# k and q of each group of four heads computed in turn, two groups inside the loop over the heads

## The chip, the cores and the metric

The kernel runs on one core of a Trainium2 chip. The metric is the time on the device in microseconds (us), lower is better. A core has TensorE (PE, matrix products; PEld is its loading of weights), VectorE (DVE), ScalarE (ACT), GpSimd (POOL) and SyncE (SP), which here only issues the loads of weights. They run side by side and meet at semaphores; each takes its own instructions strictly in order.

## What is computed

Two networks in a row on x (512 tokens, 1024 channels, float32). The first block is retention and pooling with an FFN; the second is a state space layer with an FFN, and then a layer of latent attention with an FFN. The change is in the attention layer and, by some small table work, in the FFN ahead of it:

```python
ckv = h @ w_kv_a                                   # 288 wide: 256 latent, 32 rope
c_kv = rms_norm(ckv[..., :256], kv_a_norm)
k_rope = apply_rope(rms_norm(ckv[..., 256:], k_rope_norm), cos, sin)
kv = (c_kv @ w_kv_b).reshape(b, s, 16, 128)        # per head: 64 of k, 64 of v
k_nope = rms_norm(kv[..., :64], k_nope_norm); v = kv[..., 64:]
c_q = rms_norm(h2 @ w_q_a, q_a_norm)               # 384 wide
q = (c_q @ w_q_b).reshape(b, s, 16, 96)            # per head: 64, and 32 of rope
q = concat(rms_norm(q[..., :64]), apply_rope(rms_norm(q[..., 64:]), cos, sin))
o = softmax(mask(q @ k.T / sqrt(96))) @ v          # 16 heads
x = x + o @ w_o
```

## The kernel before

Products are made in three passes from operands split in a high and a low part. A weight chunk is loaded by SP (`w_raw`), ACT makes its high part (`w_hi`, L935; for `kv_a` and `q_a` it also multiplies in the gain, L930), POOL the low part (`w_lo`, L864). ACT works up to LEAD = 4 chunks ahead of the one that TensorE is at (`ahead`), and there are six buffers for chunks. Results stand in eight PSUM banks that are used in turn; a bank can be opened when its last user is done. `rows_product` opens four banks (one for each block of 128 tokens, a tile) and goes chunk by chunk over all four; `rows_by_tile` goes tile by tile.

The attention layer runs in this order on TensorE:

1. `kv_a` (288 wide, by tile, chunks of two k) and `q_a` (384 wide, by chunk). DVE copies each result to SBUF (L1829, L1838), ACT makes the mean squares of the copy and their roots (L1190 to L1201), DVE scales (L1836, L1844). Ahead of the first of these DVE makes the angles of rope (L1821 to L1437) and ACT their sines (L1185, L1186).
2. The latents are turned (L461), scaled by their gains and split (DVE L1330, ACT L951, DVE L1299).
3. The columns: for group c = 0 to 3 (four heads each) the product `kv_b` (512 wide, two k, 24 matmuls), then for c = 0 to 3 the product `q_b` (384 wide, three k, 36 matmuls). For each tile ACT squares the result and copies it to `k_n` or `q_n` (L1232, L1234), DVE sums the squares (L1903 to L1907) and copies v (L1910). When all tiles of one product are in, ACT takes the roots (`row_deviations`, L1211, L1213) and DVE normalises (`normalised`: L1873 to L1893). Rope of q is done by POOL for groups 0 and 2 (`rope_queries`, six instructions of `rope_chunk`, L836 to L841, in POOL's queue of low parts), and by DVE inside `normalised` for groups 1 and 3.
4. The heads. Loop h does on TensorE: for each tile t the scores of head h+1 (L749) and the turning of the probabilities of head h (L759); then the turning of q and k of head h+2 (L741), and the output of head h (`head_out`, L768: ten blocks, four of them for the last tile). DVE masks the scores and takes the maxima (L1922) and copies turned probabilities of tiles 0 to 2 (`p_t`, L1937), turns out k (L1915) and writes `o_n` (L1945). ACT takes the exponentials (L1248), copies tile 3 of `p_t` (L1264) and turns out q (L1243).
5. `o_n` is turned and multiplied by w_o.

The FFN ahead of it (`f2`) needs for each of its 22 blocks f 48 matmuls of 512 columns on TensorE, for which ACT and DVE make one instruction or two each.

## Time and profile before

| | us |
|---|---|
| median of 3 runs | 1986.67 (1984.89 to 1987.19) |
| the profiled execution | 1993.77 |
| its span, first to last instruction | 1992.0 |
| TensorE busy in the span | 1831.3 (92%) |
| DVE, ACT, POOL busy | 856.4, 609.5, 679.2 |
| mean granted clock of TensorE | 0.952 |

The rows below are from the trace of that execution. In a view of stretches a row gives the stretch (us from the start of the span), its length, then the busy time and the number of instructions of PE, PEld, DVE, ACT and POOL, the clock granted to TensorE as a share of full speed, the busy share of the DMA engines and GB/s. In a timeline a row gives start, duration (of all, where several are merged), engine, line, operation, what it writes and reads, the shape, the count, and in brackets how long the engine had been idle and what ended that. TensorE has two clocks, 1.2 and 2.4 GHz, so a granted clock of 0.5 is the lower.

### The profile page before, as it was taken

What the parts mean: (1) busy time and instruction counts of PE and PEld (TensorE: products, weight loads), DVE (VectorE), ACT (ScalarE), POOL (GpSimd) and SP (SyncE); (2) the same over time, 40 slices, a digit from 0 to 9 for tenths busy, and PEclk for the clock granted to TensorE, in tenths of its full rate; (3) what the DMA queues carried; (4) which work ended last, traced back from release to release, by engine and by line L of the source; (5) the groups of instructions that cost most, each with busy time, mean ns of one, the idle gap of its engine ahead of it and who ended that gap; (6) DMA issues with size and microseconds to landing.
All of it is one profiled execution on the core that took longest, in us unless ns stands there. A gap on an engine that the chain in (4) does not pass through costs nothing.

```text
span 1992.0 us, 22762 instructions
## 1 busy us (share of the span) xinstructions
PE 1831.3 (92%) x9038; PEld 1528.2 (77%) x9038; DVE 856.4 (43%) x1644; ACT 609.5 (31%) x1006; POOL 679.2 (34%) x300
## 2 busy tenths in 40 slices
PE   5889778989899969999999999997969999999999
PEld 5677577768678748888888888887858888888887
DVE  2587668877857652541311111123676431111111
ACT  1223132313213322222432232236545433222221
POOL 1433223424423332004244343433330124535342
PEclk8899899989999978899999999999889999999999
DMA  9222144344445443632233333322200123233332
GB/s 213 56 75 74 32 130 134 122 124 137 127 127 161 144 158 107 224 141 95 74 106 96 95 91 101 99 61 87 69 31 1 33 75 106 96 98 94 100 94 80
DMA packets 234216, 202.72 MB, mean 102 GB/s; under 512 B 38912, under 2 KB 194688, under 8 KB 232064
## 3 DMA queue, kind: packets, MB, share of 16 engines
q1 hardware_dynamic: 198272, 170.29, 27.6%
q10 hardware_dynamic: 35840, 30.98, 5.2%
q8 instruction: 73, 1.20, 0.3%
q14 instruction: 31, 0.25, 0.0%
HBM read 175.55 MB, written 25.69 MB: 101 GB/s over the span
## 4 chain that ended last, share of the span: by engine, by line
PE 76%; DVE 14%; DMA 3%; ACT 2%; ACTq 2%; issue 1%; SPq 1%; POOL 1%; DVEq 0%; POOLq 0%
PE ps L347 12%; PE ps L349 12%; PE ps L348 12%; PE ps L371 8%; PE ps L372 8%; PE ps L373 8%; DMA rec<-s_records 2%; PE ps L749 2%; PE ps L768 2%; PE ps L402 1%; PE ps L403 1%; PE ps L404 1%; PE ps L665 1%; PE ps L601 1%; PE ps L759 1%
## 5 line engine op out<-in xcount | busy, mean ns | idle before, releaser
L864 POOL TENSOR_TENSOR w_lo<-w_raw,w_hi 128x1024 fp32r<-128x1024 f32 (+4 forms) x284 | 668.2, 2364 | 1272.8 <-ACT w_hi L935 1272.6
L347 PE MATMUL ps<-a_hi,w_hi 128*128 128x512 f32 (+1 forms) x1184 | 445.2, 376 | 7.9 <-DVE q_t L1558 5.5
L348 PE MATMUL ps<-a_lo,w_hi 128*128 128x512 f32 (+1 forms) x1184 | 442.8, 374 | 0.0
L349 PE MATMUL ps<-a_hi,w_lo 128*128 128x512 f32 (+1 forms) x1184 | 442.6, 374 | 0.0
L935 ACT ACTIVATE w_hi<-w_raw 128x1024 fp32r<-128x1024 f32 (+4 forms) x284 | 284.9, 1017 | 353.5 <-DMA w_raw<-in_ffn_w_gate_up_dram 72.0
L347 PEld LDWEIGHTS ps<-a_hi,w_hi 128*128 128x128 f32 x1184 | 225.0, 190 | 49.2 <-DVE q_t L1558 5.8
L349 PEld LDWEIGHTS ps<-a_hi,w_lo 128*128 128x128 f32 x1184 | 224.8, 190 | 39.4
L348 PEld LDWEIGHTS ps<-a_lo,w_hi 128*128 128x128 f32 x1184 | 225.0, 190 | 38.9
L1808 DVE TENSOR_TENSOR ev<-ps,xh 128x512 f32<-128x512 f32 x44 | 30.4, 692 | 417.6 <-PE ps L349 397.6
L371 PE MATMUL ps<-w_hi,a_hi 128*128 128x512 f32 (+1 forms) x432 | 172.6, 399 | 38.6 <-DVE a_lo L1320 12.0
L371 PE MATMUL ps<-w_hi,h_hi 128*128 128x512 f32 x476 | 189.7, 399 | 0.5 <-DVE h_lo L1320 0.5
L372 PE MATMUL ps<-w_lo,h_hi 128*128 128x512 f32 x476 | 188.6, 396 | 0.0
L373 PE MATMUL ps<-w_hi,h_lo 128*128 128x512 f32 x476 | 188.5, 396 | 0.0
L372 PE MATMUL ps<-w_lo,a_hi 128*128 128x512 f32 (+1 forms) x432 | 170.8, 395 | 0.0
L373 PE MATMUL ps<-w_hi,a_lo 128*128 128x512 f32 (+1 forms) x432 | 170.3, 394 | 0.0
L1384 DVE TENSOR_TENSOR x_rows<-ps,x_rows 128x512 f32<-128x512 f32 x72 | 48.9, 688 | 225.2 <-PE ps L373 189.2
L371 PEld LDWEIGHTS ps<-w_hi,a_hi 128*128 128x128 f32 x432 | 86.0, 199 | 55.7 <-issue 24.6
L371 PEld LDWEIGHTS ps<-w_hi,h_hi 128*128 128x128 f32 x476 | 89.8, 189 | 23.8 <-issue 2.0
L951 ACT ACTIVATE h_hi<-ev 128x512 fp32r<-128x512 f32 x66 | 41.7, 631 | 211.6 <-DVE ev L1808 195.5
L373 PEld LDWEIGHTS ps<-w_hi,h_lo 128*128 128x128 f32 x476 | 89.8, 189 | 21.7
L372 PEld LDWEIGHTS ps<-w_lo,h_hi 128*128 128x128 f32 x476 | 89.9, 189 | 21.2
L373 PEld LDWEIGHTS ps<-w_hi,a_lo 128*128 128x128 f32 x432 | 85.6, 198 | 15.2
(335 smaller groups left out, 2254.4 us busy)
## 6 DMA issues: line engine op xcount, KB each, us to landing
w_raw<-in_ffn_w_gate_up_dram SPq DMA_DIRECT2D x88, 512.0 KB, 3.8
rec<-s_records ACTq DMA_DIRECT2D x16, 1440.0 KB, 6.4
w_raw<-in_w_up_dram SPq DMA_DIRECT2D x44, 512.0 KB, 3.9
w_raw<-in_ffn_w_down_dram SPq DMA_DIRECT2D x40, 512.0 KB, 3.7
s_records<-stage SPq DMA_DIRECT2D x16, 928.0 KB, 6.1
w_raw<-in_w_in_dram SPq DMA_DIRECT2D x20, 512.0 KB, 3.9
w_raw<-in_w_down_dram SPq DMA_DIRECT2D x20, 512.0 KB, 4.0
w_raw<-in_ssm_w_glu_dram SPq DMA_DIRECT2D x16, 512.0 KB, 3.6
```

Of the source, the lines that this page charges most:

```text
L347: pe.matmul(bank, wh, xh_, start=first, stop=False)
L348: pe.matmul(bank, wh, xl_, start=False, stop=False)
L349: return pe.matmul(bank, wl, xh_, start=False, stop=last)
L371: pe.matmul(o, ah[:, k + kk, s], wh[:, kk, :], start=(n == 0 and kk == 0), stop=False)
L372: pe.matmul(o, ah[:, k + kk, s], wl[:, kk, :], start=False, stop=False)
L373: m = pe.matmul(o, al[:, k + kk, s], wh[:, kk, :], start=False, stop=end)
L749: m = pe.matmul(b[:, 0:(t + 1) * P], qk_t[:, h % 2, 0, t * P:t * P + P], qk_t[:, h % 2, 1, 0:(t + 1) * P], start=True, stop=True)
L768: m = pe.matmul(b[:, t * VD:t * VD + VD], p_t[:, o:o + P], v_n[:, j, h, :], start=(j == 0), stop=(j == t))
L864: pool.tensor_tensor(w_lo[:, n % RING, 0:w], w_raw[:, n % RING, 0:w], w_hi[:, n % RING, 0:w].bitcast(F), ALU.subtract).then_inc(lo_made, 1)
L935: act.activation(w_hi[:, n % RING, 0:w], w_raw[:, n % RING, 0:w], ACT.Copy).then_inc(hi_made, 1)
L951: act.activation(hi, view(ev[:, i % 2, :]), ACT.Copy).then_inc(hi_ready, 1)
L1384: ins = v.tensor_tensor(o, b, o, ALU.add)
```

## The change

- `kv_b` and `q_b` go in turn for a group: kv 0, q 0, kv 1, q 1 (`EARLY = 2`). The products of groups 2 and 3 stand in the loop over the heads, each after `head_out(h)`: kv 2 after head 0, q 2 after head 1, kv 3 after head 3, q 3 after head 5 (`IN_HEAD`). What ACT and DVE do for each tile of them (`evict_columns`, `column_sums`) stands at the end of their part of the same loop; the roots (`row_deviations`) stand on ACT one loop later, between the exponentials and the copy of `p_t`; `normalised` stands on DVE at the end of that later loop.
- `head_turn` waits for both products of its group only.
- `kv_a` has chunks of three k in place of two; `q_a` goes by tile. ACT squares, and DVE scales, straight out of the PSUM banks; the copies are gone.
- Angles, sines and factors of rope are made in `f2` (before f = 4, 6 and 10). The rope part of k (`k_rope`) is done after the sums of kv 0.
- POOL does the rope of q for groups 0 and 2 after the low part of one chunk past `q_b`'s, where it was two.
- The turned latents use other rows of `a_hi` and `a_lo`, and `o_n` is laid out by pairs of heads.

```diff
+EARLY = 2
+IN_HEAD = {0: (0, 2), 1: (1, 2), 3: (0, 3), 5: (1, 3)}
...
-            rows_by_tile(("kv_a",), mla_w_kv_a_2, a_hi, a_lo, KT, 0, KVR + ROPE, 2, gain=0, wait_t=mla[1],
+            rows_by_tile(("kv_a",), mla_w_kv_a_2, a_hi, a_lo, KT, 0, KVR + ROPE, 3, gain=0, wait_t=mla[1],
                          after=lambda t, n: mla[0](3) if (t, n) == (1, 1) else None)
-            rows_product("q_a", mla_w_q_a_2[0], a_hi, a_lo, KT, 0, QR, 2, gain=1)
+            rows_by_tile(("q_a",), mla_w_q_a_2[0], a_hi, a_lo, KT, 0, QR, 2, gain=1)
...
+            for c in range(EARLY):
+                columns(0, c)
+                columns(1, c)
...
             def head_turn(h):
-                pe.wait_ge(qk_rows, HC + h // HN + 1)
+                pe.wait_ge(qk_rows, 2 * (h // HN + 1))
...
                 head_out(h)
+                if h in IN_HEAD:
+                    columns(*IN_HEAD[h])
...
-                    if n == chunks_at[("q_b", c, 0)] + 2:
+                    if n == chunks_at[("q_b", c, 0)] + 1:
                         rope_queries(c)
...
+                        if (stage, f) == ("f2", 6):
+                            rope_trig()
...
             for h in range(NH):
                 for t in range(TT):
                     if h + 1 < NH:
                         exponentials(h + 1, t)
+                if h - 1 in IN_HEAD:
+                    q, c = IN_HEAD[h - 1]
+                    row_deviations(2 * c + q)
                 if h:
                     act.wait_ge(*closed(("o", h - 1)))
                 b = full(act, ("pt", h, TT - 1))
                 release(("pt", h, TT - 1), act.activation(p_t[:, tri(TT - 1)], b, ACT.Copy))
                 if h + 2 < NH:
                     q_turned(h + 2)
+                if h in IN_HEAD:
+                    q, c = IN_HEAD[h]
+                    evict_columns(2 * c + q, False)
...
+                        if (stage, f) == ("f2", 4):
+                            rope_angles()
+                        if (stage, f) == ("f2", 10):
+                            rope_factors()
...
                 v.wait_ge(*w)
+                if h - 1 in IN_HEAD:
+                    q, c = IN_HEAD[h - 1]
+                    normalised(2 * c + q)
+                if h in IN_HEAD:
+                    q, c = IN_HEAD[h]
+                    column_sums(2 * c + q, False)
```

## Rows read from the trace of the kernel before

**Rows 1.** View of stretches, core 0, the attention layer up to the last heads

```profile
1385.91:1393.14 7.23, 3.17 (x22) 2.07 (x20) 6.48 (x17) 4.10 (x11) 2.35 (x1) 0.88 0.10 27
1393.14:1400.90 7.76, 7.76 (x24) 6.18 (x25) 6.97 (x26) 3.38 (x9) 0.00 (x0) 0.67 0.00 1
...
1429.80:1433.29 3.49, 0.26 (x3) 0.03 (x1) 2.72 (x8) 3.46 (x9) 3.38 (x4) 0.86 0.73 231
1433.29:1439.60 6.31, 6.31 (x21) 6.31 (x22) 2.86 (x4) 0.29 (x1) 4.99 (x3) 0.54 0.07 27
...
1450.30:1463.65 13.35, 0.15 (x3) 0.03 (x1) 12.34 (x18) 5.59 (x13) 11.23 (x5) 0.59 0.12 38
1463.65:1470.00 6.35, 6.35 (x16) 4.25 (x17) 3.61 (x12) 3.65 (x9) 0.00 (x0) 0.51 0.00 0
1470.00:1478.97 8.97, 5.65 (x41) 4.46 (x40) 7.15 (x21) 3.53 (x10) 0.00 (x0) 1.00 0.00 0
1478.97:1562.40 83.43, 83.43 (x604) 71.08 (x604) 55.01 (x183) 45.91 (x130) 0.00 (x0) 1.00 0.01 2
```

**Rows 2.** Timeline of TensorE: two waits in the latents, two matmuls of kv_b

```profile
1349.61 0.37 PE L402 MATMUL ps<-w_hi,a_hi 128*128 128x288 f32 x1 [2.79 <-ACT w_hi L935]
...
1367.69 0.66 PE L371 MATMUL ps<-w_hi,a_hi 128*128 128x384 f32 x1 [3.82 <-POOL w_lo L864]
...
1401.30 0.39 PE L372 MATMUL ps<-w_lo,a_hi 128*128 128x512 f32 x1
...
1411.50 0.39 PE L372 MATMUL ps<-w_lo,a_hi 128*128 128x512 f32 x1
```

**Rows 3.** Timeline of ACT: the last split, a chunk of q_a, squares of two tiles

```profile
1355.48 1.09 ACT L944 ACTIVATE a_hi<-ps 128x512 fp32r<-128x512 f32 x2 [4.96 <-PE ps L427]
...
1365.56 1.11 ACT L930 ACTIVATE w_raw<-w_raw,gains 128x384 f32<-128x384 f32 x2
...
1367.44 0.40 ACT L1190 ACTIVATE xh<-ckv 128x256 f32<-128x256 f32 x1
...
1368.86 0.40 ACT L1190 ACTIVATE xh<-ckv 128x256 f32<-128x256 f32 x1
```

**Rows 4.** Timeline of POOL: low parts of q_a, and rope of group 0

```profile
1365.73 3.71 POOL L864 TENSOR_TENSOR w_lo<-w_raw,w_hi 128x768 fp32r<-128x768 f32 x2 [14.68 <-ACT w_hi L935]
...
1425.82 1.48 POOL L836 TENSOR_TENSOR q_rot<-q_n,q_trig 128x256 f32<-128x256 f32 x1 [6.06 <-ACT q_n L1234]
...
1431.33 6.95 POOL L864 TENSOR_TENSOR w_lo<-w_raw,w_hi 128x768 fp32r<-128x768 f32 x4
```

**Rows 5.** Timeline of all engines, end of one loop over the heads

```profile
1501.16 0.70 DVE L1922 CUSTOM_DVE_ANT_0 ps<-ps,mask 128x512 f32<-128x512 f32 x1 [0.15 <-PE ps L749]
...
1502.28 2.34 PE L768 MATMUL ps<-v_n,p_t 128*128 128x64 f32 x20
...
1502.63 0.59 ACT L1264 ACTIVATE p_t<-ps 128x512 f32<-128x512 f32 x1
...
1504.45 0.44 PE L749 MATMUL ps<-qk_t 96*128 96x128 f32 x2
```

**Rows 6.** Timeline of ACT: evictions of q_b, the last Sqrt, and the load behind it

```profile
1430.61 0.47 ACT L1232 ACTIVATE xh<-ps 128x384 f32<-128x384 f32 x1
...
1431.35 0.49 ACT L1232 ACTIVATE xh<-ps 128x384 f32<-128x384 f32 x1
...
1463.27 0.31 ACT L1213 ACTIVATE xh<-xh,eps_c 128x16 f32<-128x16 f32 x1
1464.49 1.28 ACT L1248 ACT_TABLE_LOAD   x1 [0.92 <-PE ps L749]
```

**Rows 7.** Timeline of DVE: normalised q of group 3, and one instruction of group 2

```profile
1459.60 2.64 DVE L1890 TENSOR_TENSOR q_n<-q_n,xh 128x512 f32<-128x512 f32 x1
...
1468.91 0.25 DVE L1873 RECIPROCAL xh<-xh 128x16 f32<-128x16 f32 x1
...
1473.29 0.69 DVE L1890 TENSOR_TENSOR q_n<-q_n,xh 128x512 f32<-128x512 f32 x1
```

More of the change, by code:

```diff
@@ L1214, in row_deviations, with evict_columns @@
                                bias=eps_c[:, 1:2]).then_inc(dev_made, 1)
-            for n in range(2 * HC):
-                q, c = divmod(n, HC)
+            def evict_columns(n, deviations):
+                c, q = divmod(n, 2)
                 for t in range(TT):
@@ L1238, in _ @@
                         ins.then_inc(k_copied, 1)
-                    if t == 1 and n:
+                    if t == 1 and deviations:
                         row_deviations(n - 1)
+            for n in range(2 * EARLY):
+                evict_columns(n, n > 0)
             def q_turned(h):
@@ L1828, in _ @@
-            for t in range(TT):
-                w = release(("kv_a", t), v.tensor_copy(ckv[:, t, :], full(v, ("kv_a", t))[:, 0:KVR + ROPE]))
-                v.wait_ge(*w)
-                v.memset(st[:, 190:191], 0.0).then_inc(lat_in, 1)
-            for t in range(TT):
-                v.wait_ge(lat_dev, t + 1)
-                step(v.reciprocal(st[:, 16 + 2 * t:18 + 2 * t], st[:, 8 + 2 * t:10 + 2 * t]))
-                c_ = ckv[:, t, 0:KVR]
-                v.tensor_scalar(c_, c_, st[:, 16 + 2 * t:17 + 2 * t], None, ALU.mult).then_inc(ckv_ready, 1)
@@ L1837, in _ @@
-            for t in range(TT):
-                w = release(("q_a", t), v.tensor_copy(cq[:, t, :], full(v, ("q_a", t))[:, 0:QR]))
-                v.wait_ge(*w)
-                v.memset(st[:, 190:191], 0.0).then_inc(lat_in, 1)
-            for t in range(TT):
-                v.wait_ge(lat_dev, TT + t + 1)
-                step(v.reciprocal(st[:, 48 + t:49 + t], st[:, 40 + t:41 + t]))
-                v.tensor_scalar(cq[:, t, :], cq[:, t, :], st[:, 48 + t:49 + t], None, ALU.mult).then_inc(cq_ready, 1)
@@ L1866, in _ @@
-            settle()
+                b = full(v, ("kv_a", t))
+                v.wait_ge(lat_dev, 2 * t + 2)
+                step(v.reciprocal(st[:, 16 + 2 * t:18 + 2 * t], st[:, 8 + 2 * t:10 + 2 * t]))
+                v.tensor_scalar(ckv[:, t, 0:KVR], b[:, 0:KVR], st[:, 16 + 2 * t:17 + 2 * t], None, ALU.mult)\
+                 .then_inc(ckv_ready, 1)
+                w = release(("kv_a", t), v.tensor_copy(ckv[:, t, KVR:], b[:, KVR:KVR + ROPE]))
+            v.wait_ge(*w)
+            for t in range(TT):
+                b = full(v, ("q_a", t))
+                v.wait_ge(lat_dev, 2 * TT + t + 1)
+                step(v.reciprocal(st[:, 48 + t:49 + t], st[:, 40 + t:41 + t]))
+                release(("q_a", t), v.tensor_scalar(cq[:, t, :], b[:, 0:QR], st[:, 48 + t:49 + t], None, ALU.mult))
@@ new lines, in _, with k_rope @@
+            split_rows("ckv_t", KVR // P, gain=kva_g, hi=c_hi, lo=c_lo)
+            split_rows("cq_t", QR // P, gain=qa_g, hi=c_hi, lo=c_lo, off=2)
+            def k_rope():
+                for t in range(TT):
+                    kr = ckv[:, t, KVR:]
+                    go(v.scalar_tensor_tensor(kr, kr, st[:, 17 + 2 * t:18 + 2 * t], hg[:, 0:ROPE], ALU.mult, ALU.mult))
+                settle()
+                k1, k2, t1, t2 = (rot[:, a, o:o + TT, :] for a in range(2) for o in (8, 12))
+                cmul(k1, k2, ckv[:, :, KVR:KVR + ROPE // 2], ckv[:, :, KVR + ROPE // 2:],
+                     trig[:, 0, :, :], trig[:, 1, :, :], t1, t2)
+                for k_, o in ((k1, NOPE), (k2, NOPE + ROPE // 2)):
+                    go(v.tensor_copy(k_n[:, :, :, o:o + ROPE // 2],
+                                     k_.unsqueeze(2).to_broadcast([P, TT, NH, ROPE // 2])))
+                settle()
@@ L1893, in normalised, with column_sums @@
                     v.tensor_tensor(x_, x_, inv(0, NOPE), ALU.mult).then_inc(qk_rows, 1)
-            for n in range(2 * HC):
-                q, c = divmod(n, HC)
+            def column_sums(n, normal):
+                c, q = divmod(n, 2)
                 for t in range(TT):
@@ L1907, in _ @@
                         v.tensor_reduce(sums(0), s3, AX.X, ALU.add).then_inc(sum_made, 1)
-                        v.wait_ge(k_copied, i + 1)
+                        v.wait_ge(k_copied, c * TT + t + 1)
                         b = full(v, ("kv_b", c, t)).rearrange("p (h e) -> p h e", h=HN)
                         release(("kv_b", c, t), v.tensor_copy(v_n[:, t, HN * c:HN * c + HN, :], b[:, :, NOPE:]))
-                    if t == 2 and n:
+                    if t == 2 and normal:
                         normalised(n - 1)
+            for n in range(2 * EARLY):
+                column_sums(n, n > 0)
+                if n == 0:
+                    k_rope()
             def k_turned(h):
@@ L1928, in _ @@
                 masked(0, t)
-            normalised(2 * HC - 1)
+            normalised(2 * EARLY - 1)
             for h in range(NH):
```

104 lines of the change are left out of this document (47 added, 57 removed).

## The prediction

> **What bounds the kernel now.** I read the view of stretches first: it shows where TensorE stands still or is slow. Then I read the timelines of each engine around those places, and last one loop over the heads, to see how much room the others have.
>
> TensorE is busy for 92% of the span, so only the places where it waits or runs at half clock can give anything. In the attention layer these are [rows 1, 2]: waits of 2.79 and 3.82 us in the latents; 7.23 us from the end of `q_a` to the first product of `kv_b` with 3.17 us of work in them; the first 7.76 us of that product at clock 0.67; a wait of about 3.5 us for a low part, and 6.31 us at 0.54 behind it; 13.35 us of standing still between the last product and the scores of head 0, while DVE works for 12.34 of them; then 6.35 us at 0.51. From 1478.97 on TensorE is busy for 83.43 of 83.43 us: the heads are bound by TensorE, and a loop takes (1504.45 − 1478.97) / 4 = 6.37 us [rows 1, 5].
>
> The products that are moved are the same matmuls before and after. They cancel; what counts is the waits around them.
>
> **In `f2`.** Angles, sines and factors go where 48 matmuls per block f hide them. A matmul of 512 takes (1411.50 − 1401.30) / 45 = 0.227 us [rows 2], so a block has 10.9 us. DVE and ACT get about 3 us each there, two table loads of 1.28 us included [rows 6], once. I cost them at nothing. Uncovered they would be 3 us.
>
> **Latents.** The copies and the sines fall away, but the chain through ACT and POOL that feeds the chunks stays.
> - `kv_a`: with three k to a chunk, 18 matmuls in place of 12 lie ahead of the third low part, which comes no sooner. The wait of 2.79 us becomes about 2.1, and the small second one goes: `kv_a` ends about 1.5 us sooner.
> - `q_a`: its fourth chunk is now wanted after 18 matmuls of tile 0, where it was wanted after 72 of all tiles. ACT reaches it only behind the squares of all four tiles of `kv_a` (1.42 us each) and two other chunks (1.88 us each) [rows 3], and POOL adds 3.71 / 2 = 1.86 us [rows 4]. Counted from the end of ACT's last split of the input, a little sooner than the 1356.57 of before, say 1355 to 1356 [rows 3]: 4 x 1.42 + 3 x 1.88 + 1.86 is 13.2, so 1368.2 to 1369.2. The first chunks keep TensorE busy to about 1364.5: a wait of 4 us, as long as the 3.82 us before. `q_a` then ends about 2 us sooner (1384 for 1385.9).
> - Behind it the last tile needs 2 us less than before for its scale, but the chunks of `q_b` 0 and `kv_b` 1 are loaded only when `q_a` frees their buffers in its last tile, and ACT waits for one of them ahead of the first split. I take `kv_b` 0 to start at 1391.7 for 1393.14: **gain 1.4 us** (bounds 0, and 4 if that load is not late).
>
> **Columns of groups 0 and 1.** From the start of `kv_b` 0 to the scores of head 0:
> - The slow start stays: 7.76 us for 24 matmuls that take 5.4 at full clock.
> - kv 0, q 0 and kv 1 follow without a wait. `k_rope` (3.3 us of DVE) lies under q 0.
> - POOL begins the rope of group 0 when q 0 is evicted, about 1.9 us after its last matmul, and needs 1431.33 − 1425.82 = 5.5 us; then comes the low part of the first chunk of q 1, 1.86 us [rows 4]. kv 1 covers 5.4 us of these 9.3 or so: a wait of 4.1 us, for 3.5 before, and the slow 6.31 us behind it stay. **Loss 0.6 us.**
> - After q 1 TensorE turns heads 0 and 1, then waits for DVE: the last sums, `normalised` of kv 1 and the turned k. That is 2.3 us of standing still for 13.35, since rope of q 1 no longer stands ahead on DVE with POOL in its way (2.64 us for an instruction that takes 0.69 alone [rows 7]). **Gain 11.0 us.**
> - The scores of head 0 were made at half clock behind the long gap (6.35 us at 0.51). DVE's masks limit them to about 2 us less. I take **1.0 us gain** (bounds 0 and 2.1).
> - The sums, roots and `normalised` of q 1 before loop 0 stay as they were for q 3.
>
> Sum up to loop 0: 1.4 − 0.6 + 11.0 + 1.0 = **12.8 us gained**.
>
> **The heads.** Here the room is small. In `head_out` the last tile starts after 6 of 10 blocks, at 1502.28 + 0.6 x 2.17 = 1503.58, and ACT's copy of `p_t` is done at 1503.22: 0.36 us of room [rows 5]. The chain ahead of it is mask 3 on DVE, exponential 3, copy on ACT; DVE has 0.15 us more. Whatever comes into that chain beyond 0.36 us (ACT) or 0.5 us (DVE) is lost by TensorE.
> - Roots stand between the exponential and the copy. A Sqrt among exponentials needs a table load, and the next Exp another: 1.28 us each [rows 6]; the Exp's hides in ACT's idle time ahead of the loop, the Sqrt's does not.
> - `normalised` stands ahead of the masks of the next loop: 1.5 us for k, 2.4 us for q of group 2, and for q of group 3 with its rope 1473.29 + 0.69 − 1468.91 = 5.1 us [rows 7].
> - Evicting a q product goes at 0.74 us a tile on ACT [rows 6], where its tiles end 0.52 us apart: ACT and DVE are some 1.5 and 1.2 us late after it. After a kv product they are in time to 0.2 us.
>
> | loop | what comes into the chain | lost |
> |---|---|---|
> | 1 | load 1.28, Sqrt 0.2, 0.2 late from kv 2, less 0.36 | 1.35 |
> | 2 | late from q 2, load for Exp not hidden (together 0.9), load and two Sqrt for q 2 | 2.4 |
> | 3 | `normalised` of q 2: 2.4 less 0.5 | 1.9 |
> | 4 | as loop 1, kv 3 | 1.35 |
> | 5 | `normalised` of kv 3: 1.5, less 0.5 and a little | 0.8 |
> | 6 | as loop 2, without the load for Exp | 2.35 |
> | 7 | `normalised` of q 3: 5.1 less 0.5, less 0.3 | 4.3 |
>
> Together **14.5 us lost** (bounds: 7.0 if only loops 3, 5 and 7 lose, and 20 with the clock, below). Loads, banks and low parts of the moved chunks come in time: they are asked for at least one loop ahead, and POOL and SP have nothing else to do there. One spot is not sure: the low parts of q 3's chunks on POOL may meet `normalised` of q 2 in loop 3, which would cost up to 2.64 − 0.69 = 2.0 us [rows 7].
>
> **Sum.** −12.8 + 14.5 = +1.7 us, on the profiled execution's 1993.77: 1995.5. The median of the runs is 7.1 us lower, and the change adds the same there: 1986.67 + 1.7 = **1988.4 us**.
>
> **Rivals.**
> - *The heads take up more.* The products in loops 0, 1, 3 and 5 give ACT and DVE some 5 to 6 us in which TensorE wants nothing of them. If the loops that stand beside them (1, 2, 4, 6) lose next to nothing, 7.0 us are lost and not 14.5: 12.8 − 7.0 = 5.8 us gained, 1980.9. Against it: TensorE takes its work in order, and the copy of `p_t` is wanted before the product, not after. It decides if the waits ahead of the last tile in loops 1, 2, 4 and 6 are under about 0.4 us. Chance 0.25.
> - *The clock falls in the heads.* After waits of 2.8 and 3.5 us TensorE ran at the lower clock for several us, 2.9 us lost in the stretch at 0.54 (6.31 x 0.46); after 2.5 us in loop 0 the clock stayed at 1.00 [rows 1, 2]. Loop 7's wait (about 3.2 us in one piece) and one of loops 2 or 6 may be long enough: +5.8 us, 1994.2. It decides from a single wait of some 3 us on. Chance 0.15.
> - *A switch of tables costs more than its load.* The row shows 0.92 us of idle time ahead of the load [rows 6]; if that belongs to the switch, four Sqrt on the path add 3.7 us: 1992.1. For it is nothing but the place of the idle time, which the row puts down to TensorE. Chance 0.08. The Trainium skill ("ScalarE: Activation LUTs", What ACT_TABLE_LOAD costs) states a drain of about 1.38 us beside each load, which by its figures would be 5.5 us on the path, an estimate, and 1994; the trace shows 1.28 us for the load alone.
> - *The front gives less.* `kv_b` 0 starts no sooner (+1.4 us) and rope on POOL, with DVE against it, holds the low part of q 1 for 2 us more (up to 2.0 as above): 1991.8. Chance 0.09.
> - The forecast itself: 0.43.
>
> **Numbers.** Less than 0.2% (4 us) is about what a measurement of this kernel cannot tell from no change. The forecast (+1.7) falls within it, 0.43; faster is the first rival, 0.25; the other three are slower, 0.32. The range reaches to both sides, as the gain (12.8) and the loss (14.5) are large sums that nearly cancel: 1979 takes in the first rival, 1996 the clock. The forecast's own range is 1984 to 1993.
>
> **What would show it.** In the profile after: `kv_b` 0 starting at about 1391 to 1392; a wait of about 4 us of TensorE for a low part behind kv 1; standing still of 2 to 3 us ahead of the scores of head 0; eight table loads between exponentials and Sqrt in the heads; waits of TensorE for `p_t` in loops 1, 2, 4 and 6, and the longest one in loop 7, all together 12 to 17 us; no wait in `f2`. It is wrong if the loops beside the products lose nothing, if the front gains far more than 12.8 us, or if the clock falls in the heads.

## The result, and the profile after

| | before | after |
|---|---|---|
| median of 14 runs each, us | 1987.49 | 1995.72 |
| ratio of times, 95% interval | | 1.0042 [1.0025, 1.0059] |
| the profiled execution, and its span, us | 1993.77, 1992.0 | 1997.75, 1995.9 |
| mean granted clock | 0.952 | 0.952 |

The change made the kernel slower by 0.42%, 8.2 us. The forecast was +1.7 us, 1988.4. The measured 1995.7 lies beyond the 4 us that stood for "no change", outside the forecast's own range (1984 to 1993), and 0.3 us inside the outer range (1979 to 1996), whose upper end stood for the rival of the falling clock. A ratio in this document is an estimate of its own over the runs, not the quotient of the two medians beside it (0.9881 and 0.9893 where they differ most). Four runs of 2145 us and more are left out of the ratios of the experiments.

The two spans differ by 3.9 us only, because the executions had already drifted apart ahead of the change: the last addition of `f2` on DVE starts at 1344.21 us before and at 1339.57 after, and those 4.6 us arise long before `f2`, where the two kernels do the same: a table load of ACT already comes at 957.63 for 962.53. So everything below is counted from that addition (the *start mark*) to the turning of `o_n` (the *end mark*). Between them lie 227.97 us before and 236.58 after: **+8.6 us**, which agrees with the medians. Three marks and the loops:

| us from the start mark | before | after |
|---|---|---|
| first product of `kv_b` | 48.93 | 46.08 |
| scores of head 0 | 119.44 | 82.64 |
| loop 0 | 15.32 | 19.20 |
| loops 1 to 8 | 6.37 each | 14.27, 9.71, 15.05, 8.53, 15.96, 9.95, 10.99, 8.05 |
| end mark | 227.97 | 236.58 |

Four products stand behind the scores of head 0 now. At full clock one of `kv_b` takes 24 x 0.227 = 5.45 us and one of `q_b` 36 x 0.173 = 6.24 us, together 23.4.

- **Front.** 119.44 − 82.64 − 23.4 = 13.4 us sooner at the scores, and loop 0 takes 19.20 − 5.45 = 13.75 us for 15.32, another 1.6: **15.0 us gained**.
- **Heads.** Loops 1 to 8 take, over 6.37 us each and the products in them, 1.66, 3.34, 3.23, 2.16, 3.35, 3.58, 4.62 and 1.68 us: **23.6 us lost**.

The page of after, busy time of the engines and the granted clock in 40 slices of 49.9 us (the heads are in the 29th to 32nd):

```profile
PE 1837.6 (92%) x9038; PEld 1530.9 (77%) x9038; DVE 852.8 (43%) x1632; ACT 614.9 (31%) x1011; POOL 674.7 (34%) x299
PEclk8899889989999978989999999999988999999999
```

The shares are those of before to a point: nothing is seen of the change in them. The clock row shows a little: the two slices of 8 in this part are the 30th and 31st, and were the 29th and 30th, so slow stretches now lie inside the heads. The view of stretches of after, the front (the columns are those of [rows 1]):

```profile
1385.65:1393.40 7.75, 7.75 (x26) 6.27 (x27) 6.69 (x15) 3.95 (x12) 0.00 (x0) 0.73 0.00 1
...
1409.88:1416.19 6.31, 6.31 (x27) 6.31 (x28) 1.06 (x3) 0.00 (x0) 6.31 (x4) 0.73 0.00 0
...
1422.21:1428.56 6.35, 6.35 (x22) 4.27 (x23) 5.14 (x15) 3.68 (x10) 0.91 (x1) 0.73 0.00 0
```

and the loops over the heads, one row for each of loops 0 to 8:

```profile
1422.21:1441.41 19.20, 16.16 (x79) 12.46 (x79) 13.38 (x39) 9.18 (x26) 0.91 (x1) 0.91 0.00 1
1441.41:1455.68 14.27, 12.84 (x84) 11.75 (x82) 6.97 (x22) 8.29 (x20) 0.00 (x0) 1.00 0.17 47
1455.68:1465.39 9.71, 6.87 (x47) 5.43 (x47) 5.79 (x20) 9.24 (x20) 7.34 (x9) 0.97 0.29 95
1465.39:1480.44 15.05, 15.05 (x71) 11.93 (x72) 9.94 (x25) 6.78 (x17) 2.07 (x1) 0.79 0.00 0
1480.44:1488.97 8.53, 6.69 (x47) 5.46 (x45) 4.57 (x17) 6.72 (x15) 0.54 (x1) 0.99 0.21 63
1488.97:1504.93 15.96, 15.96 (x82) 13.81 (x83) 7.59 (x20) 7.12 (x16) 4.19 (x2) 0.79 0.05 10
1504.93:1514.88 9.95, 7.34 (x47) 6.25 (x47) 5.41 (x19) 8.17 (x19) 0.79 (x1) 0.89 0.27 93
1514.88:1525.87 10.99, 9.03 (x48) 6.96 (x48) 8.69 (x24) 4.81 (x11) 1.56 (x1) 0.79 0.00 0
1525.87:1533.92 8.05, 8.05 (x49) 6.50 (x48) 4.55 (x14) 3.52 (x10) 0.00 (x0) 0.79 0.01 2
```

The loss has two forms. In loops 1, 2, 4 and 6, at a clock of 0.97 to 1.00 except for loop 6, TensorE is busy for less than the loop: it waits. In loops 3 and 5 it is busy from end to end (15.05 of 15.05 us in loop 3), and they are still too long: the clock is 0.79. A look at busy time alone would find nothing wrong with them. The same view cut at the slow places:

```profile
1465.39:1471.84 6.45, 6.45 (x19) 4.31 (x19) 6.18 (x15) 2.98 (x7) 2.07 (x1) 0.51 0.00 0
...
1488.97:1495.54 6.57, 6.57 (x19) 4.42 (x20) 5.45 (x13) 2.98 (x7) 1.80 (x1) 0.50 0.00 1
...
1514.88:1519.40 4.52, 4.52 (x14) 3.29 (x15) 3.90 (x9) 1.28 (x1) 1.56 (x1) 0.50 0.00 0
...
1525.87:1529.80 3.93, 3.93 (x15) 2.86 (x15) 2.57 (x10) 1.17 (x5) 0.00 (x0) 0.57 0.01 4
```

What these stretches lose against full clock is 6.45 x 0.49 + 6.57 x 0.50 + 4.52 x 0.50 + 3.93 x 0.43 = 10.4 us, and loop 6 (9.95 us at 0.89) adds about 1. The waits are in the timeline of TensorE of after (start, duration, what; in brackets the idle time and what ended it), first the front, then the heads:

```profile
1344.97 0.37 PE L403 MATMUL ps<-w_hi,a_hi 128*128 128x288 f32 x1 [1.99 <-POOL w_lo L874]
...
1363.95 0.41 PE L403 MATMUL ps<-w_hi,a_hi 128*128 128x384 f32 x1 [1.67 <-POOL w_lo L874]
...
1385.65 0.76 PE L372 MATMUL ps<-w_hi,a_hi 128*128 128x512 f32 x1 [5.42 <-DVE a_lo L1323]
...
1409.88 0.41 PE L372 MATMUL ps<-w_hi,a_hi 128*128 128x384 f32 x1 [4.84 <-POOL w_lo L874]
...
1422.21 2.09 PE L757 MATMUL ps<-qk_t 96*128 96x128 f32 x7 [2.53 <-ACT qk_t L1261]
...
1448.43 1.10 PE L776 MATMUL ps<-v_n,p_t 128*128 128x64 f32 x8 [1.44 <-ACT p_t L1285]
...
1463.87 1.10 PE L776 MATMUL ps<-v_n,p_t 128*128 128x64 f32 x8 [2.14 <-ACT p_t L1285]
...
1487.46 1.10 PE L776 MATMUL ps<-v_n,p_t 128*128 128x64 f32 x8 [1.43 <-ACT p_t L1285]
...
1513.12 1.97 PE L776 MATMUL ps<-v_n,p_t 128*128 128x64 f32 x8 [2.61 <-ACT p_t L1285]
```

The first two and 5.42 answer to [rows 2] and to the 7.23 us stretch of [rows 1]; 4.84 answers to the 3.5 us wait for a low part, 2.53 to the 13.35 us of standing still. For 2.53 the row names ACT's copy of the turned q; DVE's copies of the turned k start at 1421.37 and take 1.40 us for the two, so DVE was late too, as forecast. In the heads the copy of `p_t` (L1285, which was L1264) ends the waits, as forecast, in loops 1, 2, 4 and 6. With the smaller ones (0.30 and 0.41 in loop 2, 0.41 in loop 4, 1.16 and 0.81 in loop 7) they make 10.7 us. Waits and slow clock together are 22 of the 23.6 us.

What comes into the chain is seen on ACT, the timeline of loop 1 of after:

```profile
1446.08 0.19 ACT L1266 ACTIVATION_READ_ACCUMULATOR prob<-ps,st 128x1 f32 x1
1446.29 1.28 ACT L1226 ACT_TABLE_LOAD   x1
1447.59 0.31 ACT L1226 ACTIVATE xh<-xh,eps_c 128x16 f32<-128x16 f32 x1
1447.80 0.58 ACT L1285 ACTIVATE p_t<-ps 128x512 f32<-128x512 f32 x1
```

The load follows the last exponential with no gap, the root follows the load 0.02 us later, and the copy that TensorE waits for comes 1.5 us later than it could. There are eight such loads in the heads, each of 1.28 us. The other rows of after that answer to [rows 3, 4, 7] are ACT's split of a chunk of `kv_b`, POOL's rope of group 0 with the low parts behind it, and three instructions of DVE:

```profile
1380.16 1.06 ACT L945 ACTIVATE w_hi<-w_raw 128x1024 fp32r<-128x1024 f32 x1 [1.09 <-DMA w_raw<-in_mla_w_kv_b_dram]
```

```profile
1401.55 1.49 POOL L846 TENSOR_TENSOR q_rot<-q_n,q_trig 128x256 f32<-128x256 f32 x1 [17.92 <-ACT q_n L1248]
...
1407.94 8.29 POOL L874 TENSOR_TENSOR w_lo<-w_raw,w_hi 128x768 fp32r<-128x768 f32 x5
```

```profile
1408.01 2.27 DVE L1921 TENSOR_TENSOR q_n<-q_n,xh 128x512 f32<-128x512 f32 x1 [0.62 <-POOL q_n L851]
...
1466.04 2.50 DVE L1914 TENSOR_TENSOR q_n<-q_n,xh 128x1024 f32<-128x1024 f32 x1
...
1489.41 2.44 DVE L1924 TENSOR_TENSOR k_n<-k_n,xh 128x1024 f32<-128x1024 f32 x1
```

The last two rows are of `normalised` in loops 3 and 5. Instructions like them take 1.23 us (1426.30, 1450.39) when POOL is idle. Here POOL was making low parts of chunks of w_o beside them (1465.11 to 1467.46 and 1488.43 to 1490.77), and each took 1.2 to 1.3 us longer.

### The profile page after: what moved, and what is told of

Its sections match the earlier page's. It is cut to its first block, busy times and chain, and to the rows that moved or that the text cites. A ratio compares the mean times of both kernels' runs of the same rounds, so it can differ in the third digit from the quotient of the medians.

```text
span 1995.9 us, 22760 instructions
## 1 busy us (share of the span) xinstructions
PE 1837.6 (92%) x9038; PEld 1530.9 (77%) x9038; DVE 852.8 (43%) x1632; ACT 614.9 (31%) x1011; POOL 674.7 (34%) x299
## 4 chain that ended last, share of the span: by engine, by line
PE 74%; DVE 14%; ACT 4%; DMA 3%; ACTq 2%; issue 2%; POOL 1%; SPq 1%; DVEq 0%; POOLq 0%
PE ps L348 12%; PE ps L349 12%; PE ps L350 12%; PE ps L372 8%; PE ps L374 8%; PE ps L373 8%; DMA rec<-s_records 2%; PE ps L403 2%; PE ps L404 1%; PE ps L405 1%; PE ps L757 1%; PE ps L776 1%; PE ps L666 1%; PE ps L602 1%; DVE tmp L1440 1%
## 5 line engine op out<-in xcount | busy, mean ns | idle before, releaser
L372 PE MATMUL ps<-w_hi,a_hi 128*128 128x512 f32 (+1 forms) x400 | 161.1, 403 | 36.7 <-POOL w_lo L874 15.2
L373 PE MATMUL ps<-w_lo,a_hi 128*128 128x512 f32 (+1 forms) x400 | 159.0, 398 | 0.0
L374 PE MATMUL ps<-w_hi,a_lo 128*128 128x512 f32 (+1 forms) x400 | 158.7, 397 | 0.0
L372 PEld LDWEIGHTS ps<-w_hi,a_hi 128*128 128x128 f32 x400 | 79.2, 198 | 53.5 <-issue 20.9
L373 PEld LDWEIGHTS ps<-w_lo,a_hi 128*128 128x128 f32 x400 | 79.2, 198 | 14.6
```

The lines of the kernel that those rows point to most:

```text
L372: pe.matmul(o, ah[:, k + kk, s], wh[:, kk, :], start=(n == 0 and kk == 0), stop=False)
L373: pe.matmul(o, ah[:, k + kk, s], wl[:, kk, :], start=False, stop=False)
L374: m = pe.matmul(o, al[:, k + kk, s], wh[:, kk, :], start=False, stop=end)
```

## The experiments

Three questions were open. Is the loss in the heads that of the moved work itself, its roots, table loads and `normalised`, or does the clock add its 11 us on top, so that it could be had back alone? Which part of the change makes the gain at the front? And is the group of waits around rope on POOL, which stands in both kernels, worth more than either? Each experiment edits the changed kernel or the kernel before and is timed against the kernel before. Marks are counted from the start mark as above.

### All columns ahead of the heads

```diff
-EARLY = 2
-IN_HEAD = {0: (0, 2), 1: (1, 2), 3: (0, 3), 5: (1, 3)}
+EARLY = 4
+IN_HEAD = {}
```

> All four groups ahead of the heads, in turn (EARLY = 4, IN_HEAD empty); the rest of the change is kept. Theory A (the front is a gain of some 13 to 15 us and the heads lose all of it and more): the heads run without a wait again from loop 1 on, 6.37 us each, and the stretch from the first kv_b product to loop 1 holds two more products of each kind, 23.4 us, and a second wait for a low part behind POOL's rope with its slow clock, about 7.5 us. So 15 - 7.5 = 7 to 8 us faster than before. Theory B (the front's gain exists only because two groups are left out, since DVE and POOL are what limits the columns): the columns take as long as before, 70 us, and it is within 3 us of before.

Measured: 1978.46 against 1986.46, ratio 0.9964 [0.9950, 0.9978]. The end mark is at 220.07, 16.5 us sooner than in the changed kernel. Every loop from 1 on takes 6.37 us again: the whole 23.6 us of the heads are due to what stands in them. In its place come 7.3 us in the columns, the scores of head 0 at 113.27. The timeline of TensorE of this kernel shows where:

```profile
1383.71 0.77 PE L372 MATMUL ps<-w_hi,a_hi 128*128 128x512 f32 x1 [5.69 <-DVE ev L1354]
1407.82 0.46 PE L372 MATMUL ps<-w_hi,a_hi 128*128 128x384 f32 x1 [4.83 <-POOL w_lo L874]
1438.26 0.41 PE L372 MATMUL ps<-w_hi,a_hi 128*128 128x384 f32 x1 [4.79 <-POOL w_lo L874]
1450.62 3.29 PE L757 MATMUL ps<-qk_t 96*128 96x128 f32 x10 [2.54 <-ACT qk_t L1261]
```

The wait for rope on POOL comes a second time, for group 2. So the rest of the change is a gain (7.9 us by the end mark, for 7 to 8 expected), and moving groups 2 and 3 into the heads turns it into a loss.

### No table loads in the heads

The roots in the heads become a scaled copy, which needs no table; values of q and k of groups 2 and 3 are therefore not the reference's.

```diff
+                if n >= 2 * EARLY:
+                    if q:
+                        step(act.activation(nrm[:, 1, 2, c, :], nrm[:, 0, 2, c, :], ACT.Copy, scale=1.0 / ROPE))
+                    act.activation(nrm[:, 1, q, c, :], nrm[:, 0, q, c, :], ACT.Copy, scale=1.0 / NOPE).then_inc(dev_made, 1)
+                    return
```

> In the heads the roots of the mean squares are left out (a scaled copy stands in place of Sqrt, with no eps), so there is no load of a table; the output is not the reference's. Theory A (loads of tables and what follows from them cost most): loops 1, 4 lose nothing, loops 2 and 6 under 1 us each, no fall of the clock in loops 3 and 5, heads lose 8 to 9 us in place of 23.6: 14 us faster than the changed kernel, 6 us faster than before. Theory B (normalised on DVE is what costs, and the clock falls by itself): the clock still falls in loops 3, 5 and 8 and no more than 6 us are won on the changed kernel.

Measured: 1990.64 against 1986.46, ratio 1.0021 [1.0002, 1.0040]; end mark 230.16, 6.4 us sooner than the changed kernel, where theory A had 14 and theory B at most 6. Loops 1, 2, 4 and 6 lose 1.5 to 1.8 us less each, a little more than one load of 1.28 us and the root behind it. But the view of its stretches, loops 2 to 5, has

```profile
1451.99:1460.09 8.10, 7.02 (x47) 5.74 (x46) 5.42 (x19) 6.61 (x18) 5.73 (x7) 0.95 0.33 114
1460.09:1475.83 15.74, 15.07 (x71) 11.82 (x71) 10.96 (x25) 5.51 (x16) 4.66 (x3) 0.81 0.00 1
1475.83:1482.85 7.02, 6.61 (x47) 5.47 (x45) 4.57 (x17) 5.24 (x14) 0.54 (x1) 1.00 0.25 75
1482.85:1497.02 14.17, 13.10 (x82) 11.81 (x83) 7.35 (x20) 5.84 (x15) 4.19 (x2) 1.00 0.04 10
```

Loop 3 is slow still, at 0.81, though the only wait ahead of it is now one of 1.00 us in loop 2. Loop 5 is at full clock, and a wait of DVE's work comes out in it instead (0.26 and 0.81 us). The clock falls in loops 3, 7 and 8 and not in loop 5, which is neither theory whole. Table loads, with the roots, are 6.4 of the 23.6 us lost.

### Rope of group 3 by POOL

```diff
-                for c in range(0, HC, 2):
+                for c in (0, 2, 3):
...
-                    if c % 2:
+                    if c == 1:
                         go(rope_chunk(v, c, q_rot[:, 1, :, :, :, :], step))
...
-                        v.wait_ge(q_roped, c // 2 + 1)
+                        v.wait_ge(q_roped, {0: 1, 2: 2, 3: 3}[c])
```

> The changed kernel with the rope of q of group 3 on POOL too, so that normalised of q 3 takes 2.4 us on DVE in place of 5.1. If DVE's work at the end of a loop is lost whole: loop 7 loses 1.9 us in place of 4.6, and the clock does not fall behind it (1.7 us): 4 us faster than the changed kernel, about 0.2% slower than before. If the clock falls from other causes, loop 8 still has it and only 2.7 us are won.

Measured: 1994.23 against 1986.46, ratio 1.0044 [1.0029, 1.0060]; end mark 234.09, 2.5 us sooner than the changed kernel, where 4 were expected. Loop 8 takes 6.37 us for 8.05, so its slow stretch goes with DVE's lateness, as expected. Loop 7 takes 10.24 for 10.99: it still loses 3.9 us where 1.9 were expected, as the slow stretch at its start stays (it follows the wait of 2.61 us in loop 6) and waits of 0.49 and 0.80 us remain. DVE's `normalised` of q 3 took 4.4 us there and not 2.4: POOL's low parts had piled up behind the rope, and beside them one product took 2.65 us for 0.69. The medians do not resolve 2.5 us.

### The four products in loops 0 to 3

```diff
-IN_HEAD = {0: (0, 2), 1: (1, 2), 3: (0, 3), 5: (1, 3)}
+IN_HEAD = {0: (0, 2), 1: (1, 2), 2: (0, 3), 3: (1, 3)}
```

> The changed kernel with the four products behind heads 0, 1, 2, 3. normalised of kv 2, q 2 and kv 3 then stands ahead of a product in which TensorE wants nothing. Theory A (what is in the chain of one loop is lost in that loop, and a product hides what DVE does beside it): the 1.9 and 0.8 us of the normalised in loops 3 and 5 go; the loads of tables stay in loops 1 to 4 and q 3's 4.3 us move to loop 5: 3 us faster than the changed kernel before the clock. If the clock falls behind waits of about 2 us whatever follows, it still falls two or three times and the gain stays at 3 us; if it does not fall ahead of a product, the gain is 6 us or more.

Measured: 1988.20 against 1986.46, ratio 1.0000 [0.9985, 1.0016]; end mark 229.21, 7.4 us sooner than the changed kernel; 3 were expected, or 6 and more if the clock does not fall ahead of a product. Roots and `normalised` of one product now stand in the loop that computes the next product, so fewer loops are late, and the clock falls twice where it fell four times: loops 1 to 5 lose 1.66, 4.47, 1.69, 3.34 and 4.85 us, 16.0 for 23.6. Against the kernel before it is only even.

### Rope later in POOL's queue, in three kernels

The order of POOL's queue decides how long the low part of the next q chunk is held up behind rope (4.84 us in the changed kernel). One line, first with no columns in the heads, then in the changed kernel, and, with `+ 2` as the line removed, in the kernel before:

```diff
-                    if n == chunks_at[("q_b", c, 0)] + 1:
+                    if n == chunks_at[("q_b", c, 0)] + 3:
                         rope_queries(c)
```

> The run without columns in the heads (e1), and POOL does the rope of groups 0 and 2 after the low part of three chunks past q_b's, so both chunks of the next q_b have theirs by then. In e1 TensorE waits 4.8 us twice for a low part behind the rope, and runs at half clock for some 6 us behind each (2.9 us lost). Theory A (POOL's queue is what holds TensorE there): both waits and both slow stretches go, 12 to 15 us fewer in the columns, less what DVE then lacks at the end: 9 to 12 us faster than e1. Theory B (DVE is the limit of the columns and the waits only hid it): TensorE waits longer ahead of the scores of head 0, and under 4 us are won.

Measured: 1972.29 against 1987.72, ratio 0.9907 [0.9877, 0.9937]; end mark 213.66, 6.4 us sooner than without the later rope, between the two theories (9 to 12, and under 4). The two waits of 4.8 us have become 1.7 and 2.4 us, both for DVE's copies of v. At the first, DVE had waited 0.63 us for POOL's rope of group 0, and its product behind that took 2.85 us; at the second it was making the rope of group 1 itself, with one instruction of 2.06 us for 0.42. Ahead of the scores TensorE waits 3.46 us for 2.54. So POOL's queue held TensorE, and DVE, slowed beside POOL, is the next limit.

> The changed kernel with POOL's rope after the low part of three chunks past q_b's, in place of one. The wait of 4.84 us behind kv 1 and the slow clock after it (2.9 us) go, the heads stay as they are (23.6 us lost): 7 to 8 us faster than the changed kernel, so within 2 us of before. If DVE limits the columns there too, 3 us.

Measured: 1991.87 against 1987.72, ratio 1.0016 [0.9999, 1.0033]; end mark 233.22, 3.4 us sooner for 7 to 8 expected, or 3 if DVE is the limit. The scores of head 0 come 4.7 us sooner, and loop 0 gives 1.7 of them back (20.86 for 19.20 us). The wait of 4.84 us is gone, but TensorE waits 0.78 us ahead of the turning and 3.48 for 2.53 ahead of the scores. The slow clock behind the wait was also less than the 2.9 us that was taken over from the kernel before: 6.31 us at 0.73 is 1.7 us. Loops 1 to 8 stay as they were.

> The kernel before with one number changed: POOL's rope after the low part of three chunks past q_b's, where it is two. The second chunk of q 2 waits for its low part then, not the first, and TensorE has 4.2 us more to do ahead of it. If the wait of 3.5 us and the slow clock behind it (2.9 us) are a loss of their own, 3 to 6 us faster than before; if DVE sets the end of the columns there, as the 13.35 us of standing still say, the wait only moves and it is within 2 us of before.

Measured: 1983.38 against 1987.72, ratio 0.9976 [0.9958, 0.9995]; end mark 225.85. Scores of head 0 come 6.1 us sooner, but loops 0 and 1 take 16.23 and 9.40 for 15.32 and 6.37, at clocks of 0.71 and 0.67 for 0.80 and 1.00: of 6.1 us, 2.1 are left, about the 2 us of the second case. TensorE still stands still for 13.5 us ahead of the scores. In this wait DVE makes the rope of group 1 (1430.99 to 1439.07 with the product behind it, which takes 2.71 us), then `normalised` of q 2 (its last product 2.65 us), each slowed beside POOL, and then turns out k. Rope of group 3 comes only behind the scores, in loop 0.

### The tables back behind `f2`, and the tables alone

First the kernel with all columns ahead of the heads, its angles, sines and factors put back behind `f2`; then the kernel before with only these moved into `f2`. The core of the second:

```diff
+                        if (stage, f) == ("f2", 6):
+                            rope_trig()
...
+                        if (stage, f) == ("f2", 4):
+                            rope_angles()
+                        if (stage, f) == ("f2", 10):
+                            rope_factors()
```

> e1 with angles, sines and factors of rope back behind f2, where they stood before. If the tables' place is worth what the chain through ACT says (DVE 3 us for the angles, two loads of 1.28 us on ACT ahead of the squares and the chunks of q_a): the first kv_b product starts 3 to 4 us later than in e1, which is about where it started before. If only the by-tile order gives the gain of 2.6 us at that point: it starts within 0.5 us of e1.

Measured: 1987.20 against 1987.72, ratio 0.9996 [0.9979, 1.0012]. `kv_b` starts at 52.05, 5.7 us later than with the tables early (3 to 4 were expected), and even later than before (48.93). `q_a` goes by tile now and opens four PSUM banks at once, two of them banks of `kv_a`. The second of these is freed at 1357.51, when DVE has copied its tile. DVE waits there for ACT's root, which stands behind the sines, a table load (1349.88) and two chunks of `q_a`. Its TensorE timeline has

```profile
1357.87 0.66 PE L403 MATMUL ps<-w_hi,a_hi 128*128 128x384 f32 x1 [6.50 <-DVE ckv L1871]
```

> The kernel before with only one part of the change: angles, sines and factors of rope made in f2. With the chunks of q_a in the old order. If the tables' place is worth 5.7 us at the first kv_b product (46.4 us behind the last addition of f2 for 52.1 in the by-tile order), it starts 3 to 5 us sooner than the 48.9 of before, so at 44 to 46, and the whole is 3 to 5 us faster. If the by-tile order is a gain of its own, it starts later than 46.

Measured: 1980.32 against 1989.53, ratio 0.9961 [0.9945, 0.9976]. `kv_b` starts at 44.64, which is 4.3 us sooner than before (3 to 5 were expected) and 1.4 sooner than in the changed kernel. Its wait there is

```profile
1382.53 0.77 PE L371 MATMUL ps<-w_hi,a_hi 128*128 128x512 f32 x1 [3.98 <-DVE ev L1335]
```

So the tables in `f2` are enough for the whole gain in the latents; no gain of `q_a` by tile and `kv_a` in chunks of three is seen beside it. In this execution loops 0 and 1 gave back 2.6 us (16.14 and 8.14, at clocks of 0.71 and 0.78), so the end mark, 225.95, shows 2.0 of the gain; the medians show 9 us, more than the marks account for, and I leave that difference open.

### Rope of all groups on POOL

The best of the above, with rope of groups 1 and 3 given to POOL too. DVE's last product of a group is done at the start of the next `normalised`, so DVE doesn't stand waiting for POOL.

```diff
             def normalised(n):
 
+                finish_rope()
...
-                    if c % 2:
-                        go(rope_chunk(v, c, q_rot[:, 1, :, :, :, :], step))
-                    else:
-                        v.wait_ge(q_roped, c // 2 + 1)
                     settle()
-                    v.tensor_tensor(x_, x_, inv(2, ROPE), ALU.mult).then_inc(qk_rows, 1)
+                    rope_left.append((c, inv))
```

> e6 (all columns ahead of the heads, POOL's rope three chunks past) with the rope of all four groups on POOL; DVE multiplies the rope part by its root one step later (with the next normalised, and for group 3 at the end of loop 1). Left in e6: waits of 1.7 and 2.4 us for DVE's copies of v behind group 1's rope on DVE, a slow stretch behind the second, 3.5 us ahead of the scores of head 0, and 2.3 us in loop 0 while DVE makes the rope of group 3. If DVE is now what limits the columns, these shrink and it is 5 to 7 us faster than e6. If POOL (5.2 us of low parts and 5.5 us of rope for each group, and it blocks DVE's instructions while it works) becomes the limit, under 2 us or slower.

Measured: **1968.29 against 1989.53, ratio 0.9881 [0.9860, 0.9902]**; end mark 207.96, 20.0 us sooner than before and 5.7 sooner than with rope of two groups on POOL (5 to 7 were expected). It beats both kernels. But 1.6 us of this are chance: up to `kv_b` it is the changed kernel, and gets there at 44.52 for 46.08. Behind the same wait of 1.99 us in `kv_a` the clock fell in the changed kernel and stayed up here, as 7 us of both, the changed kernel first, show:

```profile
1344.97:1351.97 7.00, 7.00 (x43) 7.00 (x44) 2.17 (x4) 2.79 (x9) 1.83 (x1) 0.76 0.01 2
...
1347.97:1354.97 7.00, 7.00 (x54) 7.00 (x55) 3.28 (x7) 4.28 (x13) 1.85 (x1) 1.00 0.01 2
```

What TensorE still waits for, up to loop 0:

```profile
1387.09 0.76 PE L372 MATMUL ps<-w_hi,a_hi 128*128 128x512 f32 x1 [5.39 <-DVE ev L1354]
1413.32 0.47 PE L372 MATMUL ps<-w_hi,a_hi 128*128 128x512 f32 x1 [0.32 <-POOL w_lo L874]
...
1445.18 4.87 PE L757 MATMUL ps<-qk_t 96*128 96x128 f32 x10 [5.92 <-issue]
```

The waits for the low parts are down to 0.32 us here and 0.25 us at 1425.54; 5.4 us ahead of `kv_b` and 5.9 ahead of the scores remain. The row names no cause for 5.9. In it DVE's `normalised` of kv 3 (1440.69) takes 3.08 us for 1.23, beside POOL's low parts, and k is turned out behind it.

### The waits of the heads filled with work

If the clock's 11 us were a loss of their own, TensorE kept busy in the waits of loops 1, 2, 4 and 6 should win them back. It turns the identity ahead of the last tile's wait, into a part of the bank that is written afterwards:

```diff
                 for t in range(TT):
+                    if t == TT - 1:
+                        for _ in range({1: 12, 2: 19, 4: 12, 6: 19}.get(h, 0)):
+                            pe.transpose(b[:, 2 * P:3 * P], ident[:, :], ident[:, :])
                     pe.wait_ge(*freed[bank_no[("pt", h, t)]])
```

> The changed kernel, where TensorE turns the identity 12, 19, 12 and 19 times into an unused part of the bank in loops 1, 2, 4 and 6, ahead of the wait for the last tile of the probabilities (0.11 us each, 1.3 and 2.1 us, about as long as it stands still there). Theory C (standing still is what takes the clock down, and the slow stretches of 6.4, 6.6 and 4.5 us behind loops 2, 4 and 6 are half of what the heads lose): those stretches are at full clock, and the waits of DVE's normalised (1.9 and 0.8 us) show in loops 3 and 5 in their place: 5 to 7 us faster than the changed kernel. Theory D (the slow stretches come whatever TensorE does there): the same as the changed kernel, or 1 us slower.

Measured: 1994.22 against 1989.53, ratio 1.0026 [1.0009, 1.0042]; end mark 236.50, where the changed kernel has 236.58. Loops 2 to 7 of this kernel:

```profile
1452.59:1462.31 9.72, 8.96 (x67) 7.42 (x66) 5.80 (x20) 9.25 (x20) 7.35 (x9) 1.00 0.25 95
1462.31:1478.40 16.09, 13.94 (x70) 11.22 (x71) 9.75 (x25) 6.79 (x17) 2.09 (x1) 0.89 0.00 1
1478.40:1486.94 8.54, 8.01 (x59) 6.68 (x57) 4.58 (x17) 6.72 (x15) 0.54 (x1) 1.00 0.21 61
1486.94:1501.12 14.18, 13.11 (x82) 11.82 (x83) 7.36 (x20) 7.12 (x16) 4.20 (x2) 1.00 0.06 11
1501.12:1510.83 9.71, 8.77 (x67) 7.45 (x66) 5.73 (x20) 8.18 (x19) 0.55 (x1) 1.00 0.28 96
1510.83:1522.87 12.04, 8.29 (x47) 6.94 (x47) 9.24 (x24) 4.81 (x11) 1.80 (x1) 0.86 0.00 1
```

The clock did rise: 1.00 in loops 5 and 6, 0.89 for 0.79 in loop 3. But in loops 3, 5 and 7 there are waits now that were not there, or were shorter, and two of their rows are

```profile
1467.19 0.61 PE L749 MATMUL ps<-ident,q_n 128*96 128x128 f32 x4 [1.35 <-ACT prob L1269]
...
1517.97 0.61 PE L749 MATMUL ps<-ident,q_n 128*96 128x128 f32 x4 [3.61 <-ACT prob L1269]
```

Loop 5 gains 1.8 us (14.18 for 15.96), loops 3 and 7 lose 1.0 each. Theory C, with its 5 to 7 us, had the clock and the waits right in part and the time wrong; the time is that of theory D. The reading that fits both is that TensorE at half clock had been covering DVE's `normalised`: at full clock it gets to the wait sooner and stands there.

## Why it came out slower

The steps of the front came as forecast, with errors that partly cancel. In the heads the waits for `p_t` came as forecast, but the forecast had the clock stay up, and it fell. The gain was 2 us more than forecast and the loss 9 us more. That the time still lies in the outer range, by 0.3 us, is luck: its upper end was meant for two falls of the clock of 2.9 us each, not for what happened. Point by point:

- **`f2` at nothing: right.** No wait of TensorE over 0.15 us lies in it, and the stage before the start mark differs by 0.3 us. The two table loads that were counted there did not come: the sines (1041.52) follow with no load behind the one at 980.05, which was made for the Silu of the gate. In the kernel before, the sines and the roots behind them had a load each on ACT in the latents (1356.59 and 1361.84, 1.28 us each); after, both are gone, and this is part of the gain below.
- **Latents, 1.4 us: 2.85 us.** The wait in `kv_a` came (1.99 us, forecast 2.1). For `q_a` one of 4 us for a low part was forecast; it was 1.67 us, and another of 0.94 us came for a PSUM bank that DVE had to free (`ckv`, L1875), which was not forecast. The chunk of `kv_b` was late by 1.1 us on ACT, as feared. I had given the place of the tables no term of its own; the two runs on the tables show that it is worth 4.3 to 5.7 us, and that the by-tile order without it is a loss.
- **Columns, −0.6 and +11.0: together 10.4 forecast, 10.6 measured.** The wait for the low part was 4.84 us for 4.1 (and 3.23 before, as 0.26 us of the 3.49 in [rows 1] are work), standing still 2.53 for 2.3. The wait has the cause that was named, rope on POOL, which took 6.39 us (1401.55 to 1407.94) for the 5.5 of the forecast, with instructions of DVE stretched beside it. The terms 1.9, 5.5 and 1.86 less 5.4 give 3.9, not 4.1. The slow clock behind the wait cost 6.31 x 0.27 = 1.7 us where 2.9 were taken as staying, and that makes up for the longer wait. So the agreement to 0.2 us is luck in its parts.
- **Scores and loop 0, 1.0 us: 1.6 us.**
- **Heads, 14.5 us: 23.6 us. This is the term that failed**, and with it the choice of the likeliest case. By loops, forecast and measured:

| loop | 1 | 2 | 3 | 4 | 5 | 6 | 7 | 8 |
|---|---|---|---|---|---|---|---|---|
| forecast | 1.35 | 2.4 | 1.9 | 1.35 | 0.8 | 2.35 | 4.3 | 0 |
| measured | 1.66 | 3.34 | 3.23 | 2.16 | 3.35 | 3.58 | 4.62 | 1.68 |
| with the waits filled | 1.66 | 3.35 | 4.27 | 2.17 | 1.57 | 3.34 | 5.67 | 1.67 |

Three things were too small or missing:

- The loops with roots (2, 4 and 6 by 0.8 to 1.2 us each, loop 1 by 0.3): waits for the last turned head and the first scores (0.30 and 0.41 us) were left out, and after a late loop the room of 0.36 us of [rows 5] is probably no longer there to be counted a second time, which no run tested.
- Loops 3, 5 and 8, by 5.6 us together, where no wait is seen but a slow stretch. Here the rival of the falling clock came true on less than its condition: it asked for one wait of some 3 us, and the granted clock fell at 1464.88 behind a wait of 2.14 us, and at 1488.78 behind 1.43 us and within the next wait of 0.41. It forecast 5.8 us on top and a time of 1994.2. Measured were 9.1 on top of the heads' 14.5, less 2.2 of extra gain at the front, and 1995.7.
- POOL, which the forecast had idle in the heads. The low parts of w_o made DVE's `normalised` 1.3 us longer in loop 3 and 1.2 in loop 5, which is as much as loop 3 is over its forecast. But in the run with rope of group 3 on POOL these low parts came later, `normalised` of kv 3 took 1.22 us for 2.44, and loop 5 was only 0.15 us shorter (15.81 us, at 0.80). So in loop 5 it was the clock, and not the slowed DVE, that set the time. For loop 3 this stays open.

The last experiment tells how far "on top" goes. With the clock held up, loop 3 waits 1.35 + 0.81 = 2.2 us and loop 5 0.26 + 0.80 = 1.1 us, in place of the slow 3.2 and 3.3: near the 1.9 and 0.8 that `normalised` was forecast to cost. So in these loops slow clock and late DVE are not added but lie over each other; what exceeds the lateness is the clock's own. In loop 5 that was 1.8 us. In loops 3 and 7 nothing was won, because the clock fell there all the same, to 0.89 and 0.86, behind DVE's own waits. In sum nothing came back. What full clock in every loop would save was not measured.

- **Heads take up more (0.25): refuted.** The waits in loops 1, 2, 4 and 6 are 1.4 to 2.6 us, far over its 0.4.
- **A switch of tables costs more than its load: refuted.** In loop 1 the load starts where the exponential ends and the root starts 0.02 us behind it; five of the eight loads have an idle time of 0.02 us ahead of them, and the other three, all for Exp, 0.93 to 1.12 us, which ACT spends idle ahead of the next scores. The Trainium skill ("ScalarE: Activation LUTs", What ACT_TABLE_LOAD costs) adds a drain of some 1.38 us; this trace doesn't show it. By the page's sum the eight loads would take 21 us, an estimate, where the rows give 8 x 1.28 = 10.2. Four of them lay on the path, 5.1 us, and taking all away with their roots gave 6.4.
- **The front gives less: refuted,** though the low part of q 1 did come later.
- **q 3's low parts against `normalised` of q 2 (up to 2.0 us): nearly.** DVE's instruction in loop 3 took 2.50 us (1466.04), where its like in loop 7 took 1.37 and with POOL idle 1.23. What it met was not a low part of q 3 but the next one in POOL's queue, of w_o (1465.11). It stretches DVE's chain ahead of the wait in loop 3 of the last experiment too (2.53 us there).

Undoing one part at a time gives the account: all of the change but the columns in the heads is a gain (0.9964), the columns in the heads cost 23.6 us and save 7.3, and with all columns ahead of the heads the gain is 7.9 us by the marks. Of it 2.6 us come up to `kv_b`, from the tables. Another 3.6 come from there to the scores: the order kv 0, q 0 takes the standing still ahead of the scores from 13.2 to 2.5 us, but the wait behind POOL's rope comes twice, 4.8 us each, for once 3.2. Loop 0 gives 1.7.

## What to carry to other kernels

When independent work is put into a stage that TensorE already fills, count what the helpers must do for it in the chain of each loop, and count the loops behind it too: a late chain has no room left to absorb the next lateness. Before moving work off a stretch with idle time, look at what ends the idle time; here one number in the order of POOL's queue and rope on another engine were worth 1.2% together with the tables and the order of the products (chance in the clock included), where moving the products into the heads saved 7.3 us and cost 23.6 in a place without slack. And read the granted clock beside the busy share: a stage that is busy from end to end may hide a late engine at half clock, and raising the clock may then only bring the wait back.
